# Two of eight parts of y held in two PSUM banks through the expert loop

## The reference, cut to what matters

```
s1, s2 = scores of the query's two halves against 128 keys each     # per head, 8 heads
top 16 of each, top 16 of their sums  -> 16 experts of 16384, with softmax gates
act = gelu(expert_u[eid] . x)
y   = sum over heads and slots of  gate * act * expert_v[eid]        # 1024 numbers per token
x  += y
```

## Time and profile before

| | us |
|---|---|
| median of 3 runs (lowest, highest) | 1976.17 (1975.48, 1979.67) |
| the profiled execution | 1981.45 |
| its span, first to last instruction | 1979.6 |
| busy PE | 1846.8 (93%) |
| busy DVE | 1428.1 (72%) |
| busy ACT | 620.5 (31%) |
| busy POOL | 410.8 (21%) |

### The profile page before, as it was taken

The page is one execution under the profiler, slowest core; times in us unless marked ns, Lnnn a source line. Parts: engine busy times, 40 slices in busy tenths (PEclk is TensorE's granted clock), DMA queues, the critical chain, the costliest instruction groups (busy, mean ns, idle before and its releaser), DMA issues. The chain is left out here.

```text
span 1979.6 us, 27393 instructions
## 1 busy us (share of the span) xinstructions
PE 1846.8 (93%) x9305; PEld 1601.1 (81%) x9305; DVE 1428.1 (72%) x3197; ACT 620.5 (31%) x1016; POOL 410.8 (21%) x478
## 2 busy tenths in 40 slices
PE   7999689999999989977999999999999999999993
PEld 6887357446676558777999999998999999998993
DVE  2376754218999977767878878878878887876763
ACT  1212155111111146653333332332332332323332
POOL 1000100001232400013434434433333323310000
PEclk9999799999999989998999999999999999999996
DMA  9001341222221226558889878888888888865542
GB/s 346 12 17 54 121 174 63 101 100 65 75 75 44 64 88 224 213 206 291 280 266 308 302 253 303 300 268 295 303 271 293 302 273 308 284 219 157 163 134 101
DMA packets 199894, 381.89 MB, mean 193 GB/s; under 512 B 13103, under 2 KB 138989, under 8 KB 196429
## 3 DMA queue, kind: packets, MB, share of 16 engines
q1 hardware_dynamic: 161845, 243.37, 36.4%
q0 software_dynamic: 36864, 134.23, 19.4%
q10 hardware_dynamic: 1056, 2.62, 0.4%
HBM read 343.36 MB, written 35.34 MB: 191 GB/s over the span
## 5 line engine op out<-in xcount | busy, mean ns | idle before, releaser
L1286 PE MATMUL bank<-p_high,v_high 128*128 128x416 f32 x896 | 315.8, 352 | 9.8 <-DVE v_low L1696 5.2
L1286 PE MATMUL bank<-p_high,v_low 128*128 128x416 f32 x896 | 317.5, 354 | 0.0
L1286 PE MATMUL bank<-p_low,v_high 128*128 128x416 f32 x896 | 314.2, 351 | 0.0
L1238 PE MATMUL bank<-h_high,u_high 128*128 128x416 f32 x768 | 273.1, 356 | 25.9 <-DVE u_low L1696 22.2
L1238 PE MATMUL bank<-h_high,u_low 128*128 128x416 f32 x768 | 273.3, 356 | 0.0
L1238 PE MATMUL bank<-h_low,u_high 128*128 128x416 f32 x768 | 270.8, 353 | 0.0
L1467 POOL DMA_INDIRECT rows<-in_u_rows,row_u x128 | 173.3, 1354 | 262.2 <-DVE dots L1778 197.7
L1396 ACT CAST p_high<-gel 128x416 fp32r<-128x416 f32 x128 | 69.1, 540 | 475.0 <-DVE gel L1741 463.2
L1467 POOL DMA_INDIRECT rows<-in_v,row_u x128 | 149.7, 1170 | 295.8 <-DVE y L1773 226.6
L467 PE MATMUL proj<-w_in_sb,xT 128*128 128x256 f32 (+1 forms) x880 | 196.0, 385 | 14.3 <-DMA w_in_sb<-in_w_in 13.9
L467 PEld LDWEIGHTS proj<-w_in_sb,xT 128*128 128x128 f32 (+1 forms) x880 | 155.1, 177 | 53.5 <-issue 12.0
(11 more groups left out here) (218 smaller groups left out, 2808.7 us busy)
## 6 DMA issues: line engine op xcount, KB each, us to landing
vv<-in_v SPq DMA_DIRECT2D x112, 512.0 KB
u<-in_uT SPq DMA_DIRECT2D x96, 512.0 KB
gates_kept<-staged SPq DMA_DIRECT2D x13, 2048.0 KB, 7.5
gate<-gates_kept SPq DMA_DIRECT2D x30, 832.0 KB
early<-in_uT SPq DMA_DIRECT2D x32, 512.0 KB, 3.6
w_in_sb<-in_w_in SPq DMA_DIRECT2D x4, 2048.0 KB, 22.8
wq<-in_w_q SPq DMA_DIRECT2D x16, 512.0 KB, 3.6
u<-in_v SPq DMA_DIRECT2D x16, 512.0 KB
```

Source lines behind the costliest of these rows:

```text
L1238: ins = pe.matmul(a_ps[par][:, 0:DT], x[:, par, k], y, start=(k == 0 and n == 0), stop=(k == KT - 1 and n == 2))
L1286: ins = pe.matmul(y_ps[m % 4][:, 0:DT], x[:, c, at:at + P], y, start=(c == 0 and n == 0), stop=(c == CG - 1 and n == 2))
```

## The change

`y` keeps m = 0 and m = 1 in banks 4 and 5 through the whole loop: their first matmul of all carries the start flag, their last of all the stop flag, and DVE copies each bank into yT once, after the last group. The other six values of m take turns in banks 0 to 3, by a running number that is 6 per group, and are added as before. PE's wait before a summed m is for the add four summed places before; before a kept m it waits for none. `yT` is cleared for the six only.

```diff
+KEPT = 2
...
-        y_ps, a_ps, g_ps = banks[0:4], banks[6:8], banks[0:4]
+        kept_ps, y_ps, a_ps, g_ps = banks[4:4 + KEPT], banks[0:4], banks[6:8], banks[0:4]
+        SUMMED = KT - KEPT
+        assert SUMMED * GROUPS % 4 == 0
+
+        def y_bank(gg, m):
+
+            return y_ps[(SUMMED * gg + m - KEPT) % 4]
+
...
-                q = KT * g + m
...
-                wait(pe, y_added, q - 3)
+                if m >= KEPT:
+                    wait(pe, y_added, SUMMED * g + m - KEPT - 3)
+                known = isinstance(part, int)
+                opens = m >= KEPT or known and part == gg == 0
+                closes = m >= KEPT or known and (part, gg) == (PARTS - 1, GROUPS - 1)
+                out = (y_bank(gg, m) if m >= KEPT else kept_ps[m])[:, 0:DT]
...
-                        ins = pe.matmul(y_ps[m % 4][:, 0:DT], x[:, c, at:at + P], y,
-                                        start=(c == 0 and n == 0), stop=(c == CG - 1 and n == 2))
+                        ins = pe.matmul(out, x[:, c, at:at + P], y, start=(opens and c == 0 and n == 0),
+                                        stop=(closes and c == CG - 1 and n == 2))
...
-            nc.gpsimd.memset(yT[:, :, P:T], 0.0).then_inc(y_zero, 1)
+            nc.gpsimd.memset(yT[:, KEPT:KT, P:T], 0.0).then_inc(y_zero, 1)
...
             def add(part, gg, m):
-                q = KT * (GROUPS * part + gg) + m
-                wait(dve, y_added, q - KT + 1)
-                dve.wait_ge(v_done, q + 1)
+                if m < KEPT:
+                    return
+                g = GROUPS * part + gg
+                wait(dve, y_added, SUMMED * (g - 1) + m - KEPT + 1)
+                dve.wait_ge(v_done, KT * g + m + 1)
                 acc = yT[:, m, P:T]
-                nc.vector.tensor_tensor(acc, acc, y_ps[m % 4][:, 0:DT], ALU.add).then_inc(y_added, 1)
+                nc.vector.tensor_tensor(acc, acc, y_bank(gg, m)[:, 0:DT], ALU.add).then_inc(y_added, 1)
+
+            def take_kept(m):
+                dve.wait_ge(v_done, KT * (NG - 1) + m + 1)
+                nc.vector.tensor_copy(yT[:, m, P:T], kept_ps[m][:, 0:DT])
...
-            for m in range(KT):
+            for m in range(KEPT):
+                take_kept(m)
+            for m in range(KEPT, KT):
                 add(PARTS - 1, GROUPS - 1, m)
```

## The result

The changed kernel takes 1966.67 us (median of 13 runs, 1961.72 to 1973.10) against 1976.17 us before (13 runs beside them, 1972.16 to 1986.33). The ratio is 0.9943, with a 95% interval of 0.9927 to 0.996: 0.57% faster, 11.3 us, with 7.9 to 14.4 us as its edges (the two medians lie 9.5 us apart). The profiled execution took 1965.89 us, 15.6 less than the profiled one before, so the two profiles differ by more than the kernels do. Two executions at a much lower granted clock (2694.11 us at 0.651, of the kernel before, and 3134.59 us at 0.556, the profiled one of the run e6_pe_flat) count in no ratio.

The account below looks back on a forecast made before the run. The prediction took PE to bound the loop, with DVE and transfers close behind. Gains of 0.5 us (group 24) and 1.0 us (entry of group 8), 1.5 together, took 1976.17 to 1974.7 us, range 1967.0 to 1980.0.

Parts of the forecast that it names:

- PE sets the end: Whole loop: PE, busy 143.75 of 149 us, ends it; only part of its 20.2 us of waits can be won.
- The adds: DVE in the loop: 64 adds fewer at 0.49 us, 31.4 us less work; each closing copy taken as 0.58 us.
- the idle time before adds: DVE before its adds, 0.0 us before: to rise above 0.0, a sign that DVE catches up with PE.
- m = 2 of group 24: PE's 2.46 us wait for an add there: the matmul starts one add earlier, 0.5 us gained, v_low as releaser.
- The other wait for an add: PE at m = 6 of group 23: 2.0 us, needing its own group's m = 2 add before and after; gain 0.
- Entry of group 8: PE's three gaps, 5.16 us: DVE comes 1.0 us earlier, the first shrinks to 1.1, the others keep their size; gain 1.0.
- The 3.00 us is PE's own branch: 0.: PE's gap without a releaser at its branch back to group 16: unchanged, gain 0.
- Rival 4: PE's branch gap strikes a second time, at group 8, costing 6.5 us: 1981.2 us; chance 0.05.
- Groups 5, 12 and 13: PE's gaps of 1.36, 1.74 + 1.22 and 1.0 us there: DVE's lead does not reach them, gain 0.
- rival 3: Rows fetched earlier meet u and v transfers, 6.7 us slower: 1982.9; sign: waits for rows or v_high grow; chance 0.12.
- rival 1: DVE's lead of 1.0 us per group reaches every gap DVE ends, 11.0 us gained: 1965.2; chance 0.22.
- Rival 2: DVE's shorter body makes its branch back free; the three gaps at group 8 go, 5.7 us: 1970.5; chance 0.06.

Follow-up runs that it names:

- e6_pe_flat: The kernel before with PE's two hardware loops written out: 1974.84 us, ratio 0.9986 to the kernel before.
- e4_none: The kernel before without its adds except the last four, and without PE's waits for them (y not right): 1960.30 us, ratio 0.9914 to the kernel before.
- e16_dve_incs: The changed kernel with three increments of an unused semaphore on DVE in place of each left-out add: 1975.39 us, ratio 0.9993 to the kernel before.
- e1_pad: The changed kernel with a same-shape addition on unused yT, behind the old wait, for each left-out add: 1975.43 us, ratio 0.999 to the kernel before.
- e17_pe_incs: The changed kernel with three increments of an unused semaphore per group on PE: 1971.34 us, ratio 0.997 to the kernel before.
- e8_small: e1_pad with each put-back addition one column wide instead of 416: 1972.24 us, ratio 0.9974 to the kernel before.
- e5_dve_flat: The kernel before, all adds in place, with DVE's two hardware loops written out: 1971.36 us, ratio 0.9965 to the kernel before.
- e13_flat: The changed kernel with DVE's two hardware loops written out: 1967.50 us, ratio 0.995 to the kernel before.
- e2_one: The changed kernel with one value of m kept in a bank instead of two, seven rotating: 1972.53 us, ratio 0.9978 to the kernel before.
- e19_both_incs: The changed kernel with unused semaphore increments on both DVE and PE: 1976.12 us, ratio 0.9989 to the kernel before.
- e9_keep4: The changed kernel with four values (even m) kept in banks 2 to 5, odd ones rotating in two banks: 1963.31 us, ratio 0.9937 to the kernel before.

## Why the prediction was wrong, point by point

- **PE sets the end, and all that can be won is its waits and the clock behind a gap.** Right: 11.2 us of waits and 3.5 us of clock are 14.7 of the 15.7 us by which the profiled span shrank. That only a part of the 20.2 us can be won held even for e4_none, which was 16.8 us faster than the kernel before beside it.
- **The adds: 64 x 0.49 us less for DVE, the copies 0.58.** Right in size: busy time fell by 28.3 us, the copies took 583 ns. That the idle time before adds would be above 0.0 came true by the letter only: 0.5 us over 138 adds.
- **m = 2 of group 24, 0.5 us.** Right: the matmul at 1784.03 waited 1.97 us, for v_low, where it was 2.46 us for the add. The other wait for an add stayed (2.2, forecast 2.0).
- **Entry of group 8: DVE "starts group 8 at 1178.38" after 4.55 us of stop, and comes 1.0 us earlier.** This is the step that failed. The sum had the stop of DVE as fixed in length and only shifted it in time. It was 0.64 us in the changed kernel, so DVE came 3.9 us earlier than it would have, and the 5.16 us of PE's three gaps went whole instead of by 1.0. The rest of the step fits e16_dve_incs, which has the freed time and the stop: the first gap was to shrink to 1.1 (1.09 there) and the other two to keep their size (1.52 and 1.48 for 1.29 and 1.75). It is not shown by that, since e1_pad, with the time put back and a stop of 3.31, has nearly the same three, 1.12, 1.14 and 1.81 us.
- **"The 3.00 us is PE's own branch: 0."** Failed in the same way. PE's body went from 838 to 830 instructions (two waits for adds less in each of four groups), its branch took 0.22 us instead of 6.10, and the stop went, with the 3.5 us of clock behind it. Rival 4 had priced this gap at 6.5 us, as a loss if it came twice; that it might go was not on the list. e17_pe_incs puts it back alone and loses 0.27% (5.3 us), though its interval and the change's overlap at their edges.
- **Groups 5, 12 and 13: 0.** Group 13 as forecast (0.94 us before, 0.96 after), the others not: 1.36 and 1.74 + 1.22 us became nothing and 0.61. Some of it may be the lead (in group 12 the row numbers were written 8.76 us after PE had begun the group before, 6.16 after), but the load of v behind the wait for v_high in group 11 took 5.7 us after, from issue to landing, and 9.2 us before, from issue to ACT's first use of it, with the same neighbours, so chance has a part: in e8_small and e5_dve_flat group 5 has 1.57 and 1.51 us again, in e13_flat, which has the freed time, 1.37. What these groups are worth by themselves was not separated.
- **The waits for v_high grew** (57.7 to 75.9 us on DVE from 919 us on), which the prediction named as a sign of rival 3. It need not be one: a DVE that is early waits there longer, for a transfer that starts at PE's pace. Waits for rows of v grew from 8.8 to 16.2 us in 919 to 1765 us, those for rows of u fell from 11.6 to 8.9, and the median fell all the same, where rival 3 had it rise to 1982.9.

**The rivals.** The time came out near rival 1's 1965.2, but not by its mechanism: with DVE's loops written out the freed time was worth 0.09%, and with both sets of increments 0.11% (2.2 us, with 4.7 us and -0.4 us as edges) is all that was left for it and PE's rule of waiting. The forecast for these was 1.5 us. Rival 2 was the mechanism, with a chance of 0.06 and a price of 5.7 us. It had been priced at PE's gaps at group 8 alone and argued down with "eight adds are few of a body". That argument weighs the work that is left out; what counted was that every instruction behind a missing one moves: DVE's body is twenty instructions shorter, and begins and ends elsewhere. Rival 2's own reason, that the body is shorter, is not shown either, since the second loop, shorter by as much, got the stop that it had not had. The other argument, that the sequencer "still comes to the branch with nothing queued behind it", is true and explains why the stop was seen at group 8 and mostly covered at group 16, not that it stays. In the runs a branch back took DVE 0.3 us or 2.9 to 4.5, and PE 0.22 to 0.24 or 4.4 to 7.5. The Trainium skill's rule ("Runtime: NRT & Kernel Launch", section "Instruction fetch mechanics") that a taken branch outside the held pages makes an engine fetch is right in kind: the traces have stops at taken branches, and the kernels whose PE loops pass without the stop have 64 or 63 fetches where those with it have 73. The Trainium skill's 512 instructions for DVE and 2048 for PE, set beside 368 and 838 as plain lengths (1606 on PE with the weight loads), would have both bodies fit before the change as well, and yet both engines stopped.

**What is shown and what isn't.** Shown: instructions without work in DVE's body by themselves take nearly the whole gain (e16_dve_incs), taking DVE's branch away in the kernel before gives 0.35% without any change to the adds (e5_dve_flat), and the stops are the branches, by their own rows. Taken one at a time, PE's branch (0.14 or 0.15%), DVE's (0.35%) and the freed time where DVE has no branch (0.09%) come to 0.58 or 0.59%, beside the change's 0.57%; each has an interval of some 0.15% to either side. Put back one at a time they don't add up: DVE's increments cost 0.50% alone, PE's 0.27% alone, both 0.46% (0.9989 less 0.9943, some 9 us of 11). Both kernels with increments on DVE have its stop at two branches, where the kernel before has it at one and the changed one at the other, so 0.46% is not exactly the part of the branches; it may be too much. It may also be that a stop of either engine lets the other and the transfers catch up; that was only argued. The second stop is a candidate too for why e16_dve_incs lost more than e8_small with bodies of the same length (0.9993 and 0.9974): e8_small passes group 16 in 0.3 us, e16_dve_incs in 4.5, with 2.27 us of PE's waits behind it. The two intervals leave chance possible as well. Open: what of the place of the code decides whether a branch stops. Length alone doesn't: e1_pad and e16_dve_incs have bodies of the same length that begin eight instructions apart in the compiled programs, and differ at group 16. No run moved the code and changed nothing else.

## What to carry to other kernels

Before forecasting an edit inside a hardware loop, look in the trace for the branch instruction of each engine at each branch back, and for the time to the next instruction: it is a price that a few instructions more or less can switch on or off, in either direction, also at a loop further on, and here it was worth more than the work edited. It is seen in full only where nothing is queued behind it. An idle stretch without a releaser is a hint at it and no proof: e13_flat, with no branch on DVE, has one of 2.86 us before a row at 1475.03. To learn what a freed microsecond of an engine is worth, put back its time and its instructions separately; putting back both at once (e1_pad) proves whichever theory one holds. Where the code has room, writing the loop out on the engine that is late (0.35% here) takes the risk away on that engine.

## What the runs showed of the hardware that was not expected

- A branch back has two sizes and nothing between. From DVE's branch to its next instruction it is 0.3 us or 2.9 to 4.5 us, in 12 profiles with two such branches each; PE's branch takes 0.22 to 0.24 us or 4.4 to 7.5. Twenty instructions less in a body moved DVE's long one from the first loop to the second.
- The profile page's count of instruction fetches tells PE's case from outside: 73 packets in every kernel with PE's body at 838 or 839 (before, e2_one, e5_dve_flat, e17_pe_incs, e19_both_incs), 64 with 830, 63 with 814 or less, 76 with PE written out. Lengths of DVE's body don't show in it.
- Sums can stay open in a PSUM bank through 32 groups, between matmuls into other banks, at no cost that can be seen (a matmul of `weigh` takes 352 ns in the median before and after), and with two rotating banks instead of four (e9_keep4) PE waited for no add.
